# V pages multiplied in pairs, and the prompt's steps gathered at the even pages, in the head loop of a hybrid decoder step

## The reference, cut to what matters

```python
def _fox_attend(q, fq, qpos, k, v, fk, kpos):
    s = jnp.einsum('nqhd,nkhd->nhqk', q, k).astype(jnp.float32) * (HEAD_DIM ** -0.5)
    s = s + (jnp.transpose(fq, (0, 2, 1))[:, :, :, None]
             - jnp.transpose(fk, (0, 2, 1))[:, :, None, :])
    mask = kpos[None, :] <= qpos[:, None]
    s = jnp.where(mask[None, None], s, -jnp.inf)
    p = jax.nn.softmax(s, axis=-1)
    return jnp.einsum('nhqk,nkhd->nqhd', p.astype(v.dtype), v)
...
            k_past = cache_k[page_table].reshape(nb, -1, N_HEADS, HEAD_DIM)
            v_past = cache_v[page_table].reshape(nb, -1, N_HEADS, HEAD_DIM)
```

## Time and profile before

| what | value |
|---|---|
| median of 3 runs | 971.62 us (970.4 to 973.45) |
| profiled execution, its own time | 975.04 us |
| its span, first to last instruction | 973.2 us |
| mean granted TensorE clock | 0.996 |
| PE busy | 939.5 us (97%) |
| DVE, ACT, POOL busy | 486.6, 385.1, 167.4 us |
| DMA | 206.41 MB, 212 GB/s over the span |

### The profile page before, as it was taken

One profiled execution on the slowest core, in us unless ns is written; L12 is line 12 of the kernel. 1 busy time (PEld: TensorE's weight loads), 2 busy tenths in 40 slices (PEclk: granted clock), 3 DMA queues, 4 the chain that ended last, 5 costly groups with the idle time before them and its releaser, 6 DMA issues.

```text
span 973.2 us, 23705 instructions
## 1 busy us (share of the span) xinstructions
PE 939.5 (97%) x8516; PEld 802.0 (82%) x8516; DVE 486.6 (50%) x1133; ACT 385.1 (40%) x728; POOL 167.4 (17%) x111
## 2 busy tenths in 40 slices
PE   4999999999999999999999999999999999999998
PEld 4999999999998987868768778688687686776898
DVE  5675444556355334554544544645545545445632
ACT  5333333332144443543444534535434445345210
POOL 2233444332030311102002002011020020000000
PEclk9999999999999999999999999999999999999999
DMA  7233222225343527799799798798996997987412
GB/s 233 66 87 86 86 76 75 85 65 130 120 165 103 174 55 228 254 329 341 237 360 313 249 364 290 247 376 261 315 350 237 362 323 244 365 297 249 142 44 98
DMA packets 133334, 206.41 MB, mean 212 GB/s; under 512 B 8848, under 2 KB 91457, under 8 KB 133171
## 3 DMA queue, kind: packets, MB, share of 16 engines
q1 hardware_dynamic: 121602, 198.35, 60.7%
q10 hardware_dynamic: 11168, 5.51, 2.0%
q0 software_dynamic: 528, 2.10, 0.8%
HBM read 195.29 MB, written 10.63 MB: 212 GB/s over the span
## 4 chain that ended last, share of the span: by engine, by line
PE 82%; DMA 7%; ACT 4%; DVE 4%; issue 2%; SPq 1%; ACTq 0%; DVEq 0%
PE psum L1221 40%; PE psum L1201 16%; PE psum L1270 9%; PE psum L1404 7%; PE psum L1519 4%; DMA page_ring<-in_cache_k 4%; ACT sample_scores L707 2%; DMA w_raw<-in_a_w_out 2%; PE psum L1469 1%; PE psum L1447 1%; DMA residual<-in_x_prompt 1%; PE psum L1319 1%; PE psum L1427 1%; PE psum L1449 1%; DMA page_ring<-in_cache_v 1%
## 5 line engine op out<-in xcount | busy, mean ns | idle before, releaser
L1221 PE MATMUL psum<-xn_high,w_high 128*128 128x256 f32 (+1 forms) x992 | 237.2, 318 | 2.6 <-DVE w_low L832 2.6
L1221 PE MATMUL psum<-xn_low,w_high 128*128 128x256 f32 (+1 forms) x992 | 216.4, 297 | 0.0
L1221 PE MATMUL psum<-xn_high,w_low 128*128 128x256 f32 (+1 forms) x992 | 216.3, 297 | 0.0
L1221 PEld LDWEIGHTS psum<-xn_high,w_high 128*128 128x128 f32 x992 | 163.9, 191 | 20.2 <-issue 16.6
L1221 PEld LDWEIGHTS psum<-xn_high,w_low 128*128 128x128 f32 x992 | 169.0, 191 | 0.0
L1221 PEld LDWEIGHTS psum<-xn_low,w_high 128*128 128x128 f32 x992 | 168.9, 190 | 0.0
L1201 PE MATMUL psum<-constants,page_ring 128*128 128x128 f32 x1024 | 137.5, 277 | 7.7 <-DMA page_ring<-in_cache_k 6.5
L1201 PEld LDWEIGHTS psum<-constants,page_ring 128*128 128x128 f32 x1024 | 114.8, 141 | 35.1 <-issue 33.4
L501 POOL TENSOR_TENSOR w_raw<-w_raw,gains 128x1024 f32<-128x1024 f32 x32 | 60.8, 1899 | 338.9 <-DMA w_raw<-in_b_w_in 220.7
L1009 DVE COPY k_turned_odd<-psum 128x512 f32<-128x512 f32 x64 | 44.2, 691 | 93.5 <-PE psum L1201 93.5
L832 DVE TENSOR_TENSOR w_low<-w_raw,w_high 128x1024 fp32r<-128x1024 f32 x32 | 51.4, 1606 | 72.6 <-ACT w_high L565 72.6
(11 more groups left out here) (236 smaller groups left out, 1420.2 us busy)
## 6 DMA issues: line engine op xcount, KB each, us to landing
page_ring<-in_cache_k SPq DMA_DIRECT2D x128, 512.0 KB, 5.6
page_ring<-in_cache_v SPq DMA_DIRECT2D x128, 512.0 KB, 4.8
w_raw<-in_a_w_in SPq DMA_DIRECT2D x30, 512.0 KB, 4.1
suffix<-suffix_scratch SPq DMA_DIRECT2D x32, 256.0 KB, 4.8
w_raw<-in_b_w_in SPq DMA_DIRECT2D x16, 512.0 KB, 6.2
w_raw<-in_kv_w SPq DMA_DIRECT2D x16, 512.0 KB, 6.1
w_raw<-in_a_w_out SPq DMA_DIRECT2D x4, 1024.0 KB, 5.1
f_broad<-f_scratch SPq DMA_DIRECT2D x8, 512.0 KB, 6.2
```

What stands on the lines that cost most here:

```text
L1221: mm = pe.matmul(PS[:, bank + h, 0:c.stop - c.start], w[:, k, :], x[:, k, c], start=(k == 0 and n == 0), stop=(k == KT - 1 and n == 2))
```

## The change

The pages keep their order and their signals. Pages 2m and 2m + 1 now stand together, sixteen recorded matmuls in a row, and every prompt step and gate piece stands ahead of an even page. `block_out(3)` stands behind the last page.

```diff
-            steps = {0: [(block_scores, 1)], 3: [(block_turn, 0)], 4: [(block_scores, 2)], 5: [(block_out, 0)],
-                     7: [(block_turn, 1)], 8: [(block_scores, 3), (block_out, 1)], 10: [(block_turn, 2)],
-                     12: [(block_out, 2)], 13: [(block_turn, 3)], 15: [(block_out, 3)]}
+            steps = {0: [(block_scores, 1)], 4: [(block_turn, 0), (block_scores, 2)], 6: [(block_out, 0)],
+                     8: [(block_turn, 1), (block_scores, 3)], 10: [(block_out, 1), (block_turn, 2)],
+                     12: [(block_out, 2)], 14: [(block_turn, 3)]}
             for k in range(NPG):
                 for step, r in steps.get(k, []):
                     step(r)
-                if k in (1, 2, 4):
-                    project(2, [{1: 5, 2: 6, 4: 7}[k]])
+                if k in (0, 2, 4):
+                    project(2, [5 + k // 2])
...
                 mm.then_inc(b_used, 1)
+            block_out(3)
```

## The result

The changed kernel takes 964.48 us (median of 5) where the kernel before, in the same session, took 970.40: the ratio of the two is 0.9928, with a 95% interval of 0.9904 to 0.9952. That is 7.0 us gained (4.7 to 9.3) against the 971.62 of before. A second session gave 0.9932 (0.9912 to 0.9952). I had forecast 4.6 us: the direction was right and the size too small, just outside the interval.

What follows compares the result with a forecast made beforehand. PE was taken to bound V halves and K page 0's landing each turn's start; 0.98 us earlier issue less 0.32 slower landing gives 0.66, times seven boundaries 4.6 us: 971.62 to 967.0 us, range 963.5 to 974.0 for 8 in 10.

Steps and rivals of the forecast that it cites:

- What bounds the kernel: Whole kernel: PE sets its own pace inside a V half, but the next turn starts when K page 0 has landed.
- The change on PE: V half: joining pages into eight runs of two and cheaper entry save 0.65 +- 0.4 us of PE time a turn.
- From issue to landing: Turn boundary: K page 0's load takes 5.6 us instead of 5.28, so PE starts 0.66 us earlier, 4.6 us over seven.
- The sum: Whole kernel: 4.6 us gained, from the median 971.62 to a forecast of 967.0 us.
- The change on SP's queue, which decides: V half: V page 8 is free 1.36 us earlier, and SP's pace puts K page 0's issue 0.98 us earlier.
- The last turn: Last turn, with no K page following: L766 starts about where it did, 0 to 0.3 us gained.
- the rival where the landing eats the gain: Boundaries: K page 0 takes over 5.83 us to land, less than 2.9 us gained, 968.7 to 974; 24%.
- the stream of loads is the engines': Boundaries: DMA engines bind the stream, K page 0 lands 0.84 us later, 5.9 us lost, 977.5; 13%, clock case included.
- The rival that PE time counts in full: Boundaries: landings keep 5.28 us or less, each gives 0.98 us, seven give 6.9, so 964.7 us; 8%.
- The page's rate: Page loads: at 408.7 GB/s each takes 1.28 us, K page 0 some 0.2 us behind; 5.4 us gained in all.

Runs made afterwards that it cites:

- out3_behind: Against the kernel before, only block_out(3) moved behind V page 15, no pages joined; ratio to before 1.0014 (0.9996 to 1.0033).
- out1_ahead: Against the changed kernel, block_out(1) put back ahead of the pair of V pages 8 and 9, all pages still paired; ratio to before 0.9959 (0.9939 to 0.9980).
- v5_joined: Against the kernel before, block_out(0) one page later, so V page 5 joins page 4 instead of page 6; ratio to before 0.9986 (0.9967 to 1.0004).

## Why the prediction was right in kind and too small

- **What bounds the kernel.** Right: TensorE inside a V half, a page load at each boundary.
- **The change on PE.** Right. 0.65 us a turn forecast, 0.69 measured where no load was in the way, and the steps stood where they were placed. As forecast, this time did not count as such: in the changed kernel 0.89 us a turn of waiting for loads stays, of 1.17.
- **From issue to landing, the step that failed.** I set 5.6 us after the change against 5.28 now, a loss of 0.32 us. The 5.6 was right (5.60). The 5.28 was turn 3's alone; the seven boundaries of the profile have 5.52 in the mean and the second profile 5.56, and the earlier trace rows held 5.72 and 6.48. That the other four are close to the 5.28 was true, and still the mean was 0.24 higher. The loss is 0.04 to 0.08, not 0.32. With 1.03 us for the issue, the mean of seven, a boundary gives 0.97 in place of 0.66, and seven give 6.8 us. The sum should have been made with means on both sides, or with the typical value on both sides. What stays open is how firm the 5.5 of before is, since out3_behind has 5.20 at the same issues.
- **The change on SP's queue, which decides.** The place and the issue times were right (0.98 us sooner forecast, 1.03 measured, at SP's pace from V page 12 on), the cause inside it not. I had K page 0's own issue decide, and so counted on V page 8 being free early by `block_out(1)`. out1_ahead undid that step, put the issue 0.67 us later, and K page 0 landed when it had. v5_joined left K page 0's issue alone, and its V halves are 0.3 to 0.6 us shorter. What counts is that the loads of V pages 13 to 15 go out 0.85 us sooner and the queue that K page 0 stands in is sooner worked off. V page 12's, sent 0.41 sooner, landed 0.16 sooner. That my 5.6 came out to the hundredth is in part luck: I took it from single rows, and the same load takes 4.98 us in out1_ahead, by its place in the queue.
- **The last turn.** I gave it 0 to 0.3 us gained. From its mark to the end of the program the changed kernel takes 92.00 and 91.94 us, the second profile of before 91.70: 0.2 to 0.3 lost. `block_out(3)` behind the last page puts L1123 0.4 us later.
- **Two slips.** In the rival where the landing eats the gain, 0.98 - 0.55 is 0.43, not 0.41; it changes nothing. And of what the profiled execution lay above the median, turn 3's start was one part, the stretch at half clock behind the last turn another, which I overlooked.
- **The rivals.** That the stream of loads is the engines' was rejected as the slower case, and it is half true: the engines do set K page 0's landing, but it did not come 0.84 later with V page 8's load: V page 12 landed about 13 us behind the mark as before, and the loads behind it, sent sooner, landed sooner. The rival that PE time counts in full, 8%, came nearest to the size with 6.9 us, but not for its reason: landings did not keep to 5.28, and TensorE still waited at every boundary.
- **The page's rate.** By the Trainium skill, "DMA: Bandwidth & Descriptors", section "iDMA fabric", a load of a page takes 1.28 us (an estimate from its 408.7 GB/s). The landings of V page 15 and K page 0 lie 1.27 us apart in the changed kernel: the trace agrees, and the estimate from it, 5.4 us, was nearer than mine, though its loss of 0.2 us was too large as well. It pointed to the queue, which I had priced by single rows.

## What to carry to other kernels

Where a step waits for the last of several loads in a queue, ask which load ahead of it was issued late, not only when its own was. Price a boundary that occurs seven times by the mean of seven, on both sides of the sum. When a wait at a turn's end shrinks, look at what other engines do in the same place: here VectorE's 1.2 us of weight splitting was next, hidden so far, and moving it took a further 0.4 us off a turn. And when two timed results differ by a few microseconds, look whether the difference lies in the part that was edited: out1_ahead's 4 us did not.

## What the runs showed of the hardware that I had not expected

A load issued 0.67 us later landed at the same time, with 4.98 us to landing in place of 5.60: behind other loads a large part of the time from issue to landing is the queue's. V page 8's load, the first after all other page loads had landed, took 3.3 us in the mean, K page 0's 5.6. With a quarter of the bytes K page 0's took 2.3 and 2.4 us in the two orders.

An idle time of TensorE of 1.88 us behind 0.17 was followed by half clock in one profile; 1.63 behind 0.42 was not in another of the same kernel, nor 1.46 behind 1.02 in the changed one.
